# Gate and up projections of a SwiGLU FFN by seven block products instead of eight, with the hidden tiles and the residual stream sent through DRAM

## The reference

```python
x = x + mix @ w_out[l]
h = rmsnorm(x, norm_ffn_g[l])                      # x * rsqrt(mean(x^2) + eps) * g
gate, up = jnp.split(h @ w_gate_up[l], 2, axis=-1) # 1024 -> 2 x 2816
x = x + (jax.nn.silu(gate) * up) @ w_down[l]       # 2816 -> 1024
return rmsnorm(x, norm_final_g)
```

## Time and profile before

| | us |
|---|---|
| median of 3 runs | 1458.38 (1457.23 to 1459.38) |
| the profiled execution | 1458.26 |
| its span, first to last instruction | 1456.5 |
| everything ahead of the output projection | 0 to 613 |
| output projection and start of gate/up | 613 to 729 |
| FFN | 729 to 1434 |
| rest of the final norm | 1434 to 1456 |

### The profile page before, as it was taken

The page is one execution under the profiler, slowest core; times in us unless marked ns, Lnnn a source line. Parts: engine busy times, 40 slices in busy tenths (PEclk is TensorE's granted clock), DMA queues, the critical chain, the costliest instruction groups (busy, mean ns, idle before and its releaser), DMA issues.

```text
span 1456.5 us, 18955 instructions
## 1 busy us (share of the span) xinstructions
PE 1385.0 (95%) x7441; PEld 1151.8 (79%) x7441; DVE 665.3 (46%) x1011; ACT 386.1 (27%) x717; POOL 43.9 (3%) x57
## 2 busy tenths in 40 slices
PE   7999999888699999999999999999999999999994
PEld 6888887565588898888888888888888887888784
DVE  6644423787577777554443332233323342323333
ACT  6000232676123232332332211121101121112113
POOL 0000000113000100100000000000000000000000
PEclk9999999999799999999999999999999999999997
DMA  5111232000212221411011112111111111111112
GB/s 207 44 58 43 73 103 77 10 1 23 56 49 79 63 50 43 183 57 44 30 58 58 32 44 68 44 43 50 43 52 58 44 33 45 67 44 49 31 51 115
DMA packets 57132, 84.41 MB, mean 58 GB/s; under 512 B 19952, under 2 KB 36336, under 8 KB 56816
## 3 DMA queue, kind: packets, MB, share of 16 engines
q1 hardware_dynamic: 57072, 83.58, 17.5%
HBM read 69.37 MB, written 13.64 MB: 57 GB/s over the span
## 4 chain that ended last, share of the span: by engine, by line
PE 68%; DVE 2%; ACT 2%; issue 1%; DMA 1%; ACTq 0%; DVEq 0%; SPq 0%
PE bank L330 51%; PE bank L1248 4%; PE bank L344 3%; PE bank L1278 1%; PE bank L1348 1%; PE bank L1342 1%; PE bank L1390 1%; PE bank L1255 1%; PE bank L1360 1%; PE bank L1377 1%; PE bank L1364 1%; PE bank L1356 1%; PE bank L1386 1%; PE bank L1374 1%; PE bank L1339 0%
## 5 line engine op out<-in xcount | busy, mean ns | idle before, releaser
L309 DVE TENSOR_TENSOR ring_wlo<-ring_raw,ring_whi 128x1024 fp32r<-128x1024 f32 (+2 forms) x102 | 114.3, 1121 | 504.8 <-ACT ring_whi L303 504.8
L330 PE MATMUL bank<-x1hi,ring_whi 128*128 128x512 f32 x688 | 267.9, 389 | 0.2 <-DVE ring_wlo L309 0.2
L330 PE MATMUL bank<-x1lo,ring_whi 128*128 128x512 f32 x688 | 267.7, 389 | 0.0
L330 PE MATMUL bank<-x1hi,ring_wlo 128*128 128x512 f32 x688 | 267.7, 389 | 0.0
L303 ACT ACTIVATE ring_whi<-ring_raw 128x1024 fp32r<-128x1024 f32 (+2 forms) x102 | 99.1, 972 | 526.8 <-PE bank L330 503.1
L330 PEld LDWEIGHTS bank<-x1hi,ring_whi 128*128 128x128 f32 x688 | 129.1, 188 | 27.4 <-issue 0.6
L330 PEld LDWEIGHTS bank<-x1lo,ring_whi 128*128 128x128 f32 x688 | 129.1, 188 | 26.9
L330 PEld LDWEIGHTS bank<-x1hi,ring_wlo 128*128 128x128 f32 x688 | 129.1, 188 | 26.6
L330 PE MATMUL bank<-hidhi,ring_whi 128*128 128x512 f32 x308 | 120.0, 390 | 0.0
L330 PE MATMUL bank<-hidlo,ring_whi 128*128 128x512 f32 x308 | 119.9, 389 | 0.0
L330 PE MATMUL bank<-hidhi,ring_wlo 128*128 128x512 f32 x308 | 119.8, 389 | 0.0
(11 more groups left out here) (266 smaller groups left out, 1975.7 us busy)
## 6 DMA issues: line engine op xcount, KB each, us to landing
ring_raw<-in_w_gate_up SPq DMA_DIRECT2D x44, 512.0 KB, 3.5
ring_raw<-in_w_in SPq DMA_DIRECT2D x20, 512.0 KB, 3.5
ring_raw<-in_w_down SPq DMA_DIRECT2D x16, 384.0 KB, 3.1
ring_raw<-in_w_down SPq DMA_DIRECT2D x16, 320.0 KB, 2.9
xin<-in_x_t SPq DMA_DIRECT2D x8, 512.0 KB, 9.1
n_scratch<-NB SPq DMA_DIRECT2D x8, 512.0 KB, 3.2
XT<-inv_scratch SPq DMA_DIRECT2D x8, 512.0 KB, 4.1
x<-in_x_t SPq DMA_DIRECT2D x2, 2048.0 KB, 8.2
```

The source lines that it names most:

```text
L309: dve.tensor_tensor(self.ring.lo[:, s, 0:self.kt, :], self.ring.raw[:, s, 0:self.kt, :], self.ring.hi[:, s, 0:self.kt, :].bitcast(F32), AL ...
L330: mm = pe.matmul(o[:, :], wpart[:, s, k, :], apart[:, k, c], start=i == 0, stop=i == n - 1)
```

## The change

**Seven products.** Take gate and up of one hidden tile as two outputs, the first and second 512 tokens as two columns, and the first and second four k tiles as the inner dimension. That is a product of a 2x2 block matrix (weights) with a 2x2 block matrix (activations), eight block products. The changed kernel forms seven: p1 to p7, each of one weight block or sum of weight blocks with one activation block or sum of blocks, over 4 k tiles, for 512 tokens. Of the 22 hidden tiles the first two (`PLAIN`) are done as before, in the layer `GUC`; the other 20 (`PAIRS`) in seven products each.

The sums of activations (over x1 times the gain) are made once, by POOL, in place in x1 (four operations of 128x2048), and split by ACT and DVE into `thi` and `tlo`. x1 has been written to DRAM before (`x1_scratch`, one DMA for each k), and ACT has scaled it in place. The sums of weights are made for each tile by POOL (`sums`, four operations of 128x512). ACT and DVE split all seven weight operands (`high`, `low`, 128x512 each). There is one buffer for each of the seven, and its next contents may be written when its product of the tile before is done.

The products of a tile go into three banks, X, Y and Z, which alternate between two sets. X: p1, which ACT copies out, and then p2 on top of it: gate for the early tokens. Y: p6; DVE adds the copy of p1 into `gat[1]`; p7 on top; DVE adds p1 into the late half of `hid`; p4 on top; DVE adds p1 into the early half of hid. Z: p5, copied out by ACT; p3 on top; DVE adds gat[1]: gate for the late tokens. For the late half of hid, POOL adds p5, multiplies by rsb2 and multiplies by the Silu. The order on PE is p6, p5, p2, p7, p3, p1 of the next tile, p4.

**Through DRAM.** Each finished hidden tile is written to DRAM (`hid_scratch`, `spill`). The down projection runs after all 22 tiles, in three groups, `GROUPS = [6, 8, 8]`. Its tiles come back (`land_hidden`), and ACT and DVE split them (`hidden_high`, `hidden_low`). x1 is read back from DRAM after the last product (eight DMAs).

The diff, cut to its core:

```diff
-GROUPS = [6, 6, 5, 5]
+GROUPS = [6, 8, 8]
+PLAIN = 2
+PAIRS = FF // P - PLAIN
...
         def stage6_sync(sp):
...
+            for k in range(KD):
+                s = k % 2
+                if k + 4 < KD:
+                    OUT.load(sp, s, (k + 4) // 2, k + 4)
+                elif k + 4 < KD + 2:
+                    GUC.load(sp, s, 0, s * FF // P)
+                sp.wait_ge(s_x1, 2 * k + 2)
+                sp.dma_start(x_dram[:, k, :], x1[:, k, :]).then_inc(s_xs[k // 4], 16)
...
         def stage6_scalar(act):
...
+            for k in range(KD):
+                act.wait_ge(s_xs[k // 4], 64)
+                act.wait_ge(s_x1lo, k + 1)
+                act.activation(x1[:, k, :], x1[:, k, :], ACT.Copy, scale=par[:, R_N2 + k:R_N2 + k + 1]).then_inc(s_xscale, 1)
             b = N2.result(act, "col", 0)
...
+        def stage7_sync(sp):
...
+            def spill(f):
+                sp.wait_ge(s_hida, f + 1)
+                sp.wait_ge(s_hidb, f + 1)
+                sp.dma_start(h_dram[f, :, :], hid[:, :]).then_inc(s_spill, 16)
+            def land_hidden(f):
+                i, dst = landing(f)
+                sp.wait_ge(s_spill, 16 * f + 16)
+                if landed_before(f):
+                    sp.wait_ge(s_hl7, f - 2)
+                sp.dma_start(dst, h_dram[f, :, :].rearrange("p (a n) -> p a n", a=2)).then_inc(s_land[i], 16)
...
+            for n in range(PAIRS):
+                sp.wait_ge(s_alo, place["p4", n] + 1)
+                if n + 2 < PAIRS:
+                    load(n + 2)
+                elif n + 1 < PAIRS:
+                    for s in range(2):
+                        DN[0].load(sp, s, 0, s, rows=0)
+                else:
+                    for f in range(3):
+                        land_hidden(f)
+                if n:
+                    spill(n - 1 + PLAIN)
+            for f in range(3, GROUPS[0]):
+                land_hidden(f)
+            V.result(sp, "Y", PAIRS - 1)
+            for k in range(KD - 1):
+                sp.dma_start(x1[:, k, :], x_dram[:, k, :]).then_inc(s_xr2[k // 4], 16)
+            spill(PAIRS - 1 + PLAIN)
+            sp.wait_ge(s_hl7, GROUPS[0])
+            sp.dma_start(x1[:, KD - 1, :], x_dram[:, KD - 1, :]).then_inc(s_xr2[1], 16)
+            for gi, layer in enumerate(DN):
+                more = gi + 1 < len(DN)
+                for turn in range(layer.n):
+                    for s in range(2):
+                        if turn + 1 < layer.n:
+                            layer.load(sp, s, turn + 1, 2 * (turn + 1) + s, rows=first_of[gi])
...
+                    if more:
+                        f = first_of[gi + 1]
+                        if gi == 0 and turn == 0:
+                            sp.wait_ge(s_spill, 16 * FF // P)
+                        for i in range(2 * turn + 3 if turn else 0, min(2 * turn + 5, GROUPS[gi + 1])):
+                            land_hidden(f + i)
+        def stage7_gpsimd(pool):
+            a, b, c, d = x1[:, 0:4, 0:HALF], x1[:, 0:4, HALF:T], x1[:, 4:8, 0:HALF], x1[:, 4:8, HALF:T]
+            pool.wait_ge(s_xscale, 4)
+            pool.tensor_tensor(a, b, a, ALU.subtract).then_inc(s_tb, 1)
+            pool.wait_ge(s_xscale, KD)
...
+            def sums(n):
+                r = raw_tiles(n)
+                pool.wait_ge(s_raw[n % 2], 32 * (n // 2) + 32)
+                if n:
+                    pool.wait_ge(s_alo, place["p3", n - 1] + 1)
...
+                pool.tensor_tensor(sum1[:, :], r[:, 2, :], r[:, 3, :], ALU.add).then_inc(s_sums, 1)
+                pool.wait_ge(s_sums, 4 * n + 1)
+                pool.tensor_tensor(sum2[:, :], sum1[:, :], r[:, 0, :], ALU.subtract).then_inc(s_sums, 1)
...
+            for n in range(PAIRS):
+                pool.wait_ge(s_u3, n + 1)
+                pool.wait_ge(s_p5, n + 1)
+                pool.tensor_tensor(hid[:, high], hid[:, high], p5, ALU.add).then_inc(s_c22, 1)
...
+        def stage7_scalar(act):
...
+            for n in range(PAIRS):
+                more = n + 1 < PAIRS
+                if more:
+                    high("p6", n + 1)
+                else:
+                    DN[0].split_hi(act, 0, 0)
+                    hidden_high(0)
+                    hidden_high(1)
+                product_done(act, "p5", n)
+                if n:
+                    act.wait_ge(s_c22, 2 * n - 1)
+                act.activation(p5, V.bank("Z", n)[:, :], ACT.Copy).then_inc(s_p5, 1)
...
+            for gi, layer in enumerate(DN):
+                for turn in range(layer.n):
+                    if gi + 1 < len(DN):
+                        for i in range(2 * turn, 2 * turn + 2):
+                            hidden_high(first_of[gi + 1] + i)
+                    for s in range(2):
+                        if turn + 1 < layer.n:
+                            layer.split_hi(act, s, turn + 1)
...
+        def stage7_vector(dve):
...
+            gate(0)
+            GUC.split_lo(dve, 0, 1)
+            moved_low(1, 1, x1[:, 0:4, 0:HALF])
+            moved_low(2, 2, x1[:, 0:4, HALF:T])
+            up_(0)
+            GUC.split_lo(dve, 1, 1)
...
+            for n in range(PAIRS):
...
+                dve.tensor_tensor(gat[1][:, :], y, p1[n % 2], ALU.add).then_inc(s_u2, 1)
+                low("p4", n)
...
+                product_done(dve, "p7", n)
+                dve.wait_ge(s_spill, 16 * f)
+                dve.tensor_tensor(hid[:, highs], y, p1[n % 2], ALU.add).then_inc(s_u3, 1)
...
+        def stage7_tensor(pe):
...
+            def product(j, n):
+                pe.wait_ge(s_alo, place[j, n] + 1)
+                name = CHAIN[j]
+                b, opens = V.bank(name, n), j in ("p1", "p6", "p5")
+                if opens:
+                    V.claim(pe, name, n)
+                else:
+                    pe.wait_ge({"p2": s_p1, "p7": s_u2, "p3": s_p5, "p4": s_u3}[j], n + 1)
...
+                for k in range(4):
+                    for i, (w, m) in enumerate(((whi, bhi), (whi, blo), (wlo, bhi))):
+                        mm = pe.matmul(b[:, :], w[:, k, :], m[:, k, :], start=opens and k == 0 and i == 0,
+                                       stop=not (j, n) in parts and k == 3 and i == 2, skip_group_check=True)
```

More of the change, by code:

```diff
@@ L299, in split_hi @@
                     self.follows.J.result(act, f"{s}1", turn - 1)
+                elif isinstance(turn, int) and turn == 0 and self.prev is not None:
+                    self.prev.J.result(act, f"{s}1", self.prev.n - 1)
                 elif not first:
-                    act.wait_ge(full[2 * s + 1], self.J.before(f"{s}1", turn))
+                    act.wait_ge(full[self.J.bank_of[f"{s}1"]], self.J.before(f"{s}1", turn))
                 act.activation(self.ring.hi[:, s, 0:self.kt, :], self.ring.raw[:, s, 0:self.kt, :], ACT.Copy
@@ new lines, in hybrid_block @@
+        count_products()
+        for n in range(PAIRS):
+            gu_order += [(name, n, b + 4 * (n % 2 == 0)) for b, name in enumerate(("X", "Y", "Z"))]
+        V = Plan(gu_order)
+        CHAIN = {"p1": "X", "p2": "X", "p6": "Y", "p7": "Y", "p4": "Y", "p5": "Z", "p3": "Z"}
+        DN, f0 = [], 0
+        for gi, G in enumerate(GROUPS):
+            DN.append(Layer(ring2, w_down, G, KD // 2, banks=(0, 1, 2, 3) if gi else (4, 5, 6, 7), prev=DN[-1] if gi else GUC))
+        first_of = [sum(GROUPS[:gi]) for gi in range(len(GROUPS) + 1)]
@@ L1816, in ff_tensor @@
                 else:
                     for s in range(2):
-                        GU.products(pe, s, 0, x1hi, x1lo)
-                with pe.Fori(1, G) as i:
+                        layer.products(pe, s, 0, hi, lo, ready if s == 0 else None)
+                for turn in range(1, layer.n - last):
                     for s in range(2):
-                        GU.products(pe, s, i, x1hi, x1lo)
-                DN.products_late(pe, 0, hidhi, hidlo, lambda k: pe.wait_ge(s_hl7, tiles0 + k + 2))
@@ L1823, in ff_tensor @@
-                with pe.Fori(1, DN.n - last) as i:
-                    for s in range(2):
-                        DN.products(pe, s, i, hidhi, hidlo)
-                if last:
-                    for s in range(2):
-                        first_half_tensor(pe, 4 * s)
-                        DN.products(pe, s, DN.n - 1, hidhi, hidlo)
-            following[gi] = GU
-            ends.append(DN)
-            return ff_sync, ff_scalar, ff_vector, ff_tensor
-        following, ends, groups = {}, [], []
@@ L1859, in stage7_tensor @@
-        def stage7_tensor(pe):
-            for g in groups:
-                g[3](pe)
+                        layer.products(pe, s, turn, hi, lo)
+            for s in range(2):
+                first_half_tensor(pe, 4 * s)
+                DN[-1].products(pe, s, DN[-1].n - 1, *HID[-1])
         s_gf, s_sq8, s_sum, s_rms, s_inv, s_fa, s_fb, s_out = (
@@ L1958, in _ @@
             def _(pool):
[L1959 removed]
+                for stage in (stage2_gpsimd, stage3_gpsimd, stage5_gpsimd, stage7_gpsimd):
                     stage(pool)
```

432 lines of the change are left out of this document (322 added, 110 removed).

## The result

The kernel before ran in 1458.37 us (median of 20 runs, 1455.14 to 1460.34) and the changed one in 1462.78 (20 runs, 1458.22 to 1467.51). The ratio is 1.0031, 95% interval 1.0022 to 1.0039: slower by 0.3%. The forecast was 1413.4 with a range of 1404 to 1437; both its sign and its range missed. The profiled execution of the changed kernel took 1462.1 us, its span is 1460.3 (before 1456.5).

The account below looks back on a forecast made before the run. The prediction took PE's matmuls as the bound, busy 95% of the span. It summed -54.4 - 3.0 + 2.6 + 0.9 + 7.0 + 2.0 = -44.9, so 1458.3 became 1413.4 us, with a range of 1404 to 1437.

Parts of the forecast that it names:

- The matmuls: FFN gate and up: 20 tiles cost 84 matmuls instead of 96, at 0.2267 us each, removing 54.4 us.
- The waits of before: PE's four waits in the old FFN for late hidden tiles, said to disappear, saving 3.0 us.
- The pair in the steady state: Each seven-product tile was to run at PE's 19.04 us, tightest at p4 with 4 us of cover; added cost 0.
- POOL: Its 128x512 operations in the pairs: 1.05 us each; with DVE's two-SBUF-input operations they share 14.3 of 19.0 us.
- rival C: In the pairs, POOL's shared load with DVE becomes the bound from 1.7 us per operation; up to 1520 us; chance 0.08.
- the signs that the prediction named for being wrong: Pairs over 19.3 us, PE wait on hid or spill, POOL operations over 1.7, no border gap, or a second gap.
- Rival A: In the pairs, the spill comes too late for p4 as transfers don't overlap: 1.2 us each, 1436 us; chance 0.16.
- Start of the pairs: Between norm 2 and the first pair: PE 2.6 us late, diagonals taken as not held; upper bound 9.
- the clock term: After the gap in the down projection's start, PE runs four microseconds at 1.2 GHz, losing 2.0 us.
- The border: From the pairs to the down projection: PE idles 7.0 us as weights and landings queue behind x1 reads and a spill.
- The first border cost: In the last pair, p3 starts 0.9 us late because ACT does two hidden highs before its copy of p5.
- Rival B: The passage from pairs to down projection costs nothing, since landings overtake the x1 reads: 1403.5 us; chance 0.09.

Follow-up runs that it names:

- the last version: Changed kernel with spill before loads, scalings spread over stage 6 with POOL's later long operations delayed, and the border's last spill ahead of all x1 reads: 1405.34 us, ratio 0.9626.
- experiment 1: Changed kernel with SP issuing each hidden tile's spill ahead of the next pair's two weight loads and the wait for p4's low: 1423.82 us, ratio 0.9749.
- Experiment 6: Changed kernel with POOL's first long sum over x1 waiting for DVE's eight diagonals of norm 2: 1461.09 us, ratio 1.0023 to the kernel before.
- experiment 3: Changed kernel with POOL's seven operations per pair cut to 8 of 512 columns from the second pair on, for timing only: 1428.68 us, ratio 0.9793.

## Why the prediction was wrong

- **The matmuls**, -54.4: right, by the 240 that are gone and the last version's busy time. The waits of before were worth 4.6 and not 3.0.
- **The pair in the steady state**: this step failed. The prediction said "4 us of cover" and took 0 per pair; measured were 40.1 us over the 20. I followed one pass, from "t = 4.2, up to 5" to PE's coming at 16.3, and asked if each thing was in time for PE. I didn't ask when t = 4.2 itself moves: DVE's low of p4 stands behind the write of hid that the previous spill releases. That write, DVE's queue, SP's two loads and the spill form a ring with none of PE's products in it, and its length, 21.0, is the period. Priced from rows of before it would have been: twelve DVE operations at 0.684 = 8.2, and an estimated 6.6 for three transfers from the earlier trace rows: 14.8 plus the issues, below 19.04. The 6.6 was right (6.3), DVE's 8.2 was 13.5. So the ring had to be drawn, and then DVE's part in it priced as held.
- **POOL**, 1.05 each taken, and the pair checked as a sum, 14.3 < 19.0: the sum was the wrong test. One operation takes 1.29 alone and 1.6 to 1.74 as it alternates. The total load still fits (experiment 1 runs at 19.13), but where POOL works at the same moment as DVE, an operation of DVE with two SBUF inputs costs up to 1.78 in the ring and not 0.68. From x = 1.7 rival C was to decide by the pair's load; what decided was the same lock, by latency and at a smaller x (1.61 in the mean of the 140). Of the signs that the prediction named for being wrong, two came true, pairs over 19.3 us and a PE wait named after hid, and a third in part: the last two of POOL's four sums take 1.68 to 1.74 in the mean.
- **Rival A** had the place right (the spill too late for p4) and the cause and price wrong: 1.2 a pair from transfers that don't overlap. They overlap (a landing of 6.3, not 11.8); measured 2.1 a pair. It had a chance of 0.16, and its 1436 was short of the result by 27.
- **Start of the pairs**: this step failed too. "I take them as not held", with 9 as an upper bound. Experiment 6 shows that the diagonals are held: 1.66 without POOL beside them, 13.29 with it. The rival reading stood in the text, with the earlier trace rows as the only row, and no row of before spoke for the choice I made. The Trainium skill (SBUF — State Buffer, Who interferes with whom) says that a tensor_scalar can enter a 2-port mode, in which it contends with GpSimd. This case's runs agree that it is held; which mode it was in no run shows. POOL's long operation is 4.55 to 4.59 us, where I took 3.7 as the most. The Trainium skill (GPSIMD Engine Reference, 3.1) gives 4497 ns for a tensor_tensor of 2048 columns, and the trace agrees. PE's stall is 9.8, and its clock then stood at 0.50 from 733 to about 737, which is about 2 more; the clock term was not in my upper bound. With the rest 12.6 in all.
- **The border**: right in mechanism and nearly in size. Gap 7.9 for 7.0; the mean clock 0.62 from 1209 to 1213, about 2 us as taken. The first border cost, "0.9", stands among the pairs' waits and measured 2.5. Rival B is refuted: the spill took 11.0 us behind seven reads of x1, 8.1 behind four of them and two weight loads, and 3.0 with all the reads behind it, and the landings wait for it.
- That the versions with pairs, start and border all mended give 1405 to 1409 does not make the forecast right: it left out what the change as written cost.

What stays open: what would become of the start with POOL's long work moved elsewhere altogether, what made three of the four runs of experiment 3 slower than the profiled one, and which step of the last chain to the border's gap could still be shortened.

## What to carry to other kernels

When a buffer is written, spilled and written again, follow the release back to the same instruction one round earlier and add up the ring, with each instruction that stands in the queues of its engines; here that ring and not the busiest engine set the period. Put the transfer that frees a buffer first in its queue, or give it a second buffer: here either brought the pair back to PE's time. Work given to POOL was cheap by load and dear by latency: a DVE operation with two SBUF inputs beside it took up to 2.6 times its own time (1.78 for 0.68).

## What the runs showed of the hardware

- DVE and POOL in alternation: a 128x512 operation of DVE with two SBUF inputs goes from 0.68 to as much as 1.78, POOL's from 1.29 to between 1.62 and 1.74; one of each takes about 1.70 us (909.27 to 910.97). A DVE operation with one operand in PSUM stays at 0.68.
- A 128x128 tensor_scalar of DVE with its input in SBUF (0.275 us in the median) was held for nearly as long as a POOL operation of 128x2048 lasts: up to 4.52 us, against 4.55 to 4.59.
- A 512 KB spill lands in 2.6 us alone, 3.0 ahead of two loads of 512 KB, 6.3 behind two, 7.2 behind two and a transfer from DRAM to DRAM, 8.1 and 9.9 behind four reads and two weight loads (one kernel, two profiles), 11.0 behind seven reads.
- PE's granted clock was at 0.50 when PE went on at 733, after its waits of 6.8 and 3.0 us for the diagonals, and at 1.00 from 738.
